# Scaled attention output in a second buffer, and the first two row blocks of the pooling difference split into a place of their own

## What is computed

```python
h = rms_norm(x, norm_mix)
q, k, v, u, ga, gp = jnp.split(h @ w_in, SPLITS, axis=-1)
o = attention_fn(q, k, v, lam)                                # (b, t, 8 heads, 128)
o = (rms_norm(o, head_norm) * (1.0 - lam_init)).reshape(b, t, ATTN_WIDTH)
pool_o, pool_state = pool_mixer(u, pool_prefix, p0, w_pool, pool_scale)
merged = jax.nn.sigmoid(ga) * (o @ w_attn_branch) + jax.nn.sigmoid(gp) * (pool_o @ w_pool_branch)
x1 = x + merged @ w_out

def pool_mixer(...):            # for each of 4 groups of 256 channels, window w = 2, 4, 8, 16
    d = ((hi - lo) / cnt - ext[...]).astype(u.dtype)          # mean of the window minus the token
    outs.append(jnp.einsum('btc,cd->btd', d, w_pool[g]) * pool_scale[g])
```

## Time and profile before

| | us |
|---|---|
| median of 3 runs | 2158.81 (2157.7 to 2162.5) |
| the profiled execution, its own time | 2162.38 |
| its span, first to last instruction | 2160.6 |
| TensorE busy | 2096.9 (97%) |
| mean granted TensorE clock | 0.994 |

### The profile page before, as it was taken

The page is one execution under the profiler, slowest core; times in us unless marked ns, Lnnn a source line. Parts: engine busy times, 40 slices in busy tenths (PEclk is TensorE's granted clock), DMA queues, the critical chain, the costliest instruction groups (busy, mean ns, idle before and its releaser), DMA issues.

```text
span 2160.6 us, 34490 instructions
## 1 busy us (share of the span) xinstructions
PE 2096.9 (97%) x13501; PEld 1907.2 (88%) x13501; DVE 1067.6 (49%) x1389; ACT 671.2 (31%) x1322; POOL 503.2 (23%) x382
## 2 busy tenths in 40 slices
PE   6999999999999999999999999999999999999998
PEld 6788888888888887899999887999999899999996
DVE  5566667666310101266773433555555555555555
ACT  4344454444443333224112311311221122122120
POOL 5423333332010101332331100311221221122120
PEclk9999999999999999999999999999999999999999
DMA  5222111222367886211124420201110111111112
GB/s 154 58 56 58 40 55 34 56 60 75 126 225 269 285 279 221 84 50 55 59 78 130 123 88 1 70 20 60 50 40 30 54 55 41 31 49 60 31 39 94
DMA packets 174539, 186.00 MB, mean 86 GB/s; under 512 B 8239, under 2 KB 147259, under 8 KB 174402
## 3 DMA queue, kind: packets, MB, share of 16 engines
q1 hardware_dynamic: 163786, 175.21, 26.0%
q10 hardware_dynamic: 10624, 8.92, 1.2%
HBM read 161.09 MB, written 23.24 MB: 85 GB/s over the span
## 4 chain that ended last, share of the span: by engine, by line
PE 85%; issue 6%; DVE 3%; POOL 2%; DMA 1%; ACT 1%; SPq 0%; ACTq 0%; POOLq 0%; DVEq 0%
PE PS L1362 33%; PE PS L2017 12%; PE PS L913 8%; PE PS L279 4%; PE PS L281 4%; PE PS L280 4%; PE PS L1839 4%; PE PS L313 3%; PE PS L337 3%; PE PS L968 3%; PE PS L326 2%; PE PS L983 2%; PE PS L1022 1%; POOL fw_lo L1349 1%; PE PS L292 1%
## 5 line engine op out<-in xcount | busy, mean ns | idle before, releaser
L1349 POOL TENSOR_TENSOR fw_lo<-fw_raw,fw_hi 128x1024 fp32r<-128x1024 f32 x86 | 215.7, 2508 | 883.0 <-ACT fw_hi L1345 838.4
L1362 PE MATMUL PS<-m_hi,fw_hi 128*128 128x384 f32 (+1 forms) x1032 | 228.4, 329 | 3.1 <-issue 1.8
L1362 PE MATMUL PS<-m_lo,fw_hi 128*128 128x384 f32 (+1 forms) x1032 | 227.4, 328 | 0.0
L1362 PE MATMUL PS<-m_hi,fw_lo 128*128 128x384 f32 (+1 forms) x1032 | 227.4, 328 | 0.0
L2144 DVE TENSOR_TENSOR x<-x,PS 128x512 f32<-128x512 f32 x198 | 135.9, 688 | 141.0 <-PE PS L2017 140.9
L279 PE MATMUL PS<-w_hi,act_hi 128*128 128x384 f32 (+1 forms) x520 | 188.2, 362 | 0.0
L1362 PEld LDWEIGHTS PS<-m_hi,fw_hi 128*128 128x128 f32 x1032 | 175.8, 188 | 4.1 <-issue 2.4
L281 PE MATMUL PS<-w_hi,act_lo 128*128 128x384 f32 (+1 forms) x520 | 176.7, 340 | 0.0
L1362 PEld LDWEIGHTS PS<-m_hi,fw_lo 128*128 128x128 f32 x1032 | 176.3, 188 | 0.0
L1362 PEld LDWEIGHTS PS<-m_lo,fw_hi 128*128 128x128 f32 x1032 | 176.2, 188 | 0.0
L280 PE MATMUL PS<-w_lo,act_hi 128*128 128x384 f32 (+1 forms) x520 | 176.1, 339 | 0.0
(11 more groups left out here) (261 smaller groups left out, 4288.5 us busy)
## 6 DMA issues: line engine op xcount, KB each, us to landing
k_pg<-in_cache_k_dram SPq DMA_DIRECT2D x64, 512.0 KB, 4.8
v_pg<-in_cache_v_dram SPq DMA_DIRECT2D x64, 512.0 KB, 5.2
fw_raw<-in_w_up_dram SPq DMA_DIRECT2D x44, 512.0 KB, 4.1
fw_raw<-in_w_in_dram SPq DMA_DIRECT2D x24, 512.0 KB, 4.8
wd_raw<-in_w_down_dram SPq DMA_DIRECT2D x22, 512.0 KB, 4.1
w_raw<-in_w_in_dram SPq DMA_DIRECT2D x21, 512.0 KB, 5.3
out_dram<-raw SPq DMA_DIRECT2D x16, 512.0 KB, 3.7
ga_scratch<-ga_ring ACTq DMA_DIRECT2D x8, 544.0 KB, 7.1
```

The source lines that it names most:

```text
L1349: e.tensor_tensor(fw_lo[slot][:, 0:kts, :], fw_raw[:, 0:kts, :], fw_hi[slot][:, 0:kts, :].bitcast(F32), ALU.subtract).then_inc(fw_tail, 1)
L1362: ins = e.matmul(PS[:, 3 * slot + c, 0:cw], w[slot][:, kt, :], x[:, kt, c0:c0 + cw], start=first and kt == 0, stop=last and kt == KT - 1)
```

## The change

Three things are done.

1. `d_first`, a pair of buffers (hi and lo) of two row blocks each, is placed in the region of the u buffers. Row blocks 0 and 1 of dT are split into it and not over `act_hi` / `act_lo`; TensorE's pool map reads them there.
2. ACT's copies of these two blocks are put ahead of the last gate (they stay behind `fm_head(N_PL)`), and DVE's subtractions of them are put ahead of `dve_normalize_o(0)`. The wait on the stores of the pooling state (`ur_st`) moves ahead of the first write to `po_lo`.
3. The scaled attention output goes to `o_sq`; the transposes read `o_sq`, and SP waits for `scaled_o` in place of `o_tr` before it loads the next block.

```diff
+        D_FIRST = 2
+        d_first = [at(f"d_first{i}", [P, D_FIRST, TOK], F32R, R2U + fit(TOK) + i * fit(D_FIRST, TOK)) for i in range(2)]
...
+        def d_parts_of(kt):
+
+            return d_first if kt < D_FIRST else (act_hi, act_lo)
...
                 e.wait_ge(d_tail, kt + 1)
-                for w, x, first, last in ((w_h, act_hi, True, False), (w_h, act_lo, False, False), (w_l, act_hi, False, True)):
+                d_hi, d_lo = d_parts_of(kt)
+                for w, x, first, last in ((w_h, d_hi, True, False), (w_h, d_lo, False, False), (w_l, d_hi, False, True)):
...
-                    ins = e.transpose(PS[:, 6 + half, j * P:j * P + n_rows], o_tile[0:n_rows, h * P:(h + 1) * P],
+                    ins = e.transpose(PS[:, 6 + half, j * P:j * P + n_rows], o_sq[0:n_rows, h * P:(h + 1) * P],
...
-            gate(N_GP + 1, KT - 1, 1)
-            e.wait_ge(d_done, KT)
...
-                    e.activation(act_hi[:, kt, :], dT[:, kt, :], ACT.Copy).then_inc(d_head, 1)
-
-            d_parts(range(5))
+                    e.activation(d_parts_of(kt)[0][:, kt, :], dT[:, kt, :], ACT.Copy).then_inc(d_head, 1)
+
+            e.wait_ge(d_done, KT)
+            d_parts(range(D_FIRST))
+            gate(N_GP + 1, KT - 1, 1)
+            d_parts(range(D_FIRST, 5))
...
-            v = o.rearrange("p (h d) -> p h d", h=NH)
-            e.tensor_tensor(v, v, rst[0:n_rows, 0, 0:NH].unsqueeze(2).to_broadcast([n_rows, NH, VD]), ALU.mult).then_inc(scaled_o, 1)
+            v, scaled = [x[0:n_rows, :].rearrange("p (h d) -> p h d", h=NH) for x in (o_tile, o_sq)]
+            e.tensor_tensor(scaled, v, rst[0:n_rows, 0, 0:NH].unsqueeze(2).to_broadcast([n_rows, NH, VD]), ALU.mult).then_inc(scaled_o, 1)
...
                 dve_pool_tile(e, step, m)
+            for kt in range(D_FIRST):
+                dve_d_tail(e, kt)
             dve_normalize_o(e, step, 0, NSAMP)
+            for kt in range(D_FIRST, 5):
+                dve_d_tail(e, kt)
             e.wait_ge(ur_st, UR_STORES * 16)
-            for kt in range(5):
-                dve_d_tail(e, kt)
...
             with e.Fori(0, KT - 1) as i:
-                e.wait_ge(o_tr, i * 2 + 2)
+                e.wait_ge(scaled_o, i + 1)
                 e.dma_start(o_tile[:, :], o_dram[bass.ds(i * P, P), :]).then_inc(o_ld, 16)
...
-            e.wait_ge(o_tr, 2 * TT - 2)
+            e.wait_ge(scaled_o, TT - 1)
             e.dma_start(o_tile[:, :], o_dram[SEQ - P:SEQ, :]).then_inc(o_ld, 16)
```

More of the change, by code:

```diff
@@ L1679, in dve_d_tail @@
             e.wait_ge(d_head, kt + 1)
-            e.tensor_tensor(act_lo[:, kt, :], dT[:, kt, :], act_hi[:, kt, :].bitcast(F32),
+            d_hi, d_lo = d_parts_of(kt)
+            e.tensor_tensor(d_lo[:, kt, :], dT[:, kt, :], d_hi[:, kt, :].bitcast(F32),
                             ALU.subtract).then_inc(d_tail, 1)
```

## The result

| | before | after |
|---|---|---|
| median, 11 runs each | 2160.81 us (2156.85 to 2166.34) | 2166.81 us (2164.77 to 2170.43) |
| span of the profiled execution | 2160.6 | 2165.1 |
| mean granted clock | 0.994 | 0.993 |

The changed kernel takes 1.0025 times as long (95% interval 1.0014 to 1.0035), 5.4 us more by that ratio; the two medians lie 6.0 us apart. The forecast was 2165.7 and +6.9. All ratios are of fast executions; one of the twelve of e4_copies_first, 2933.7 us long at a mean granted clock of 0.655, is slow and left out.

A forecast was written before the change was run, and what follows sets the result against it. TensorE, busy for 97% of the span, was taken as the bound. Pool map +6.0, clock +0.9 and early load 0 gave +6.9 us, added to the 2158.8 median: 2165.7 us, range 2161.0 to 2168.6.

The forecast's parts named there:

- The chain on DVE: Sample block: two subtractions follow ACT's copies and end at 997.8; normalization starts then, 14.0 us later, its scaling at 1002.6.
- The meeting with POOL: Sample block's scaling on DVE runs into POOL's fw_lo and takes 3.41 us in place of 1.22.
- Start of the transposes: Sample block's transposes on TensorE start at 1006.05 in place of 996.84; the pool map at 1006.65, +6.0 us.
- The clock: Half clock behind TensorE's gap loses 2.4 us, against 1.5 behind the present gap: +0.9, bounds 0 and +3.3.
- The early load: Prompt-block loop: SP issues the o_tile load 1.3 us sooner, but nobody waits for it: 0 us.
- The sum: Whole kernel: +6.0 for the pool map, +0.9 for the clock, 0 for the load: +6.9 us, 2165.7 us.
- the loop is not bound by the load: Denies the rival that the load bound the prompt-block loop and TensorE's 3.5 us of waits could go: 2162.2, 7%.
- POOL and DVE do meet: Denies the rival that they don't meet at the sample block's scaling as in the loop: 2164.0 to 2165.2 us, 12%.
- The one in which the change does what it is shaped for: Rival: subtractions and normalization done by 996.8, pool map at 997.5, no half clock: 2154.2 us, chance 4%.
- its condition: For that rival, ACT's w_pool hi part must begin at 987.0 for an equally early pool map; rows show 993.09.

The follow-up runs named there:

- e4_copies_first: Changed kernel with the sample block's normalization ahead of dT's subtractions on DVE, and ACT's two d_first copies ahead of w_pool's hi part; ratio to before 0.9975.
- e7: Kernel before with one wait added: in the prompt-block loop POOL begins each fw_lo only when DVE has scaled the block; ratio to before 0.9989.
- e10: Kernel before with POOL's fw_lo put ahead of the root in the loop over prompt blocks; ratio to before 0.9999.
- e3_norm_first: Changed kernel with the sample block's normalization put ahead of the subtractions of dT on DVE again; ratio to before 0.9980.

## Why the prediction was right

Step by step, counted from ACT's hi part of w_pool:

- *The chain on DVE.* The copies, the subtractions and the normalization follow as forecast: the square starts after 4.50 us (4.7 forecast), the scaling 4.77 us later, as in the earlier trace rows.
- *The meeting with POOL.* 3.35 us, 3.41 forecast; POOL came first by 0.07 us again, and the run with fw_lo ahead of the root shows that the meeting is its cause. All nine scalings of the kernel after are between 3.35 and 3.42 us.
- *Start of the transposes.* After 12.72 us, 12.96 forecast; the pool map after 13.73, 13.56 forecast, since the transposes themselves ran at half clock and took 1.0 and not 0.6 us.
- *The clock.* 2.6 us in this execution, 2.4 forecast. The 2.4 came from the kernel's start, another place, and that it fits is in part luck. What I subtracted for the kernel before, 1.5, was 1.6 in its profile (47.28 against 45.70 in the run with the output kept beside), but this is not a fixed price. In that run the gap in front of the pool map was 3.07 us too and no half clock came behind it:

```profile
1000.66 0.73 PE L1378 MATMUL PS<-act_hi,fw_hi 128*128 128x384 f32 x3 [3.07 <-DVE act_lo L1680]
...
1001.72 0.66 PE L1378 MATMUL PS<-act_hi,fw_lo 128*128 128x384 f32 x3
1002.22 0.66 PE L1378 MATMUL PS<-act_hi,fw_hi 128*128 128x384 f32 x3
```

  In the profile of before the same matmuls are 0.9 us apart, and so they are in the two other runs that keep this gap, e7 and e10 (their first block comes at 45.8 all the same, since the wait ahead of its transposes is gone). The price behind the long gap varies as well: 54.16 and 53.25 us to the first block in two executions with the same order. In both the clock was down for some 10 us, but it fell 4.5 us ahead of the transposes in the first and 6.5 in the second, so that 5.7 and 3.7 us of work met half clock. So the term was right for the two profiled executions that it compares; over the profiles at hand it is 0 or about 1.5 before and 1.6 to 2.6 after, and what decides within that is not shown.
- *The early load.* 0 forecast and 0 measured. One reading on the way was wrong: that ACT needs the weights load behind `o_tile` only 5 us later. ACT stands idle for it in the kernel before,

```profile
1047.05 1.06 ACT L1345 ACTIVATE fw_hi<-fw_raw 128x1024 fp32r<-128x1024 f32 x1 [3.06 <-DMA fw_raw<-in_w_pool_branch_dram]
```

  and it costs nothing there only because POOL makes the root ahead of fw_lo. With the other order on POOL this load is what decides.
- *The sum.* 6.9 us at the first block, as forecast; 4.5 in the two spans, with 1.5 us gained ahead of the change's place and 0.9 behind it, in stretches with the same work. The ratio's interval is 3.0 to 7.6 us. That the forecast time, 2165.7, is only 1.1 us from the median of 2166.81 is luck in part: it was added to the median of three runs, 2158.81, which is 2.0 us below that of the eleven, and the forecast difference is 0.9 us above that of the medians.

The rivals that were tested fell: the loop is not bound by the load, POOL and DVE do meet. The one in which the change does what it is shaped for was priced about right: the run with the copies first gains 5.4 us, and the 4.6 forecast for that case is within its interval. But its condition was too narrow. It named only the moment at which ACT begins with w_pool's hi part, and e3_norm_first gains 4.3 us with that moment unchanged, by the order on DVE alone. No run has an earlier hi part with DVE's order as changed.

## What to carry to other kernels

A step that is put ahead of another on an in-order engine brings its own wait with it: before splitting a wait off, look at what releases the moved instruction (here ACT behind a weight load), and at how much slack the instructions behind it had (here 7 us, all of it used). A loop that waits for one engine can be held up by a second one whose instructions exclude the first one's, and which of the two orders is better depends on when the data for them is loaded. An edit that is worth nothing alone can be what another one needs.

## What the runs showed of the hardware

- A POOL subtraction of two SBUF inputs and a DVE instruction of two SBUF inputs did not run at once in any of the rows read here: DVE took 3.35 to 3.42 us in place of 1.22 where POOL's 2.40 us began first, and POOL took 3.29 in place of 2.40 where DVE's square began first. DVE's reduction (one input) ran beside it at its usual 1.22 us.
- The same gap of 3.07 us on TensorE was followed by half clock in three profiles and by none in one; it cost about 1.5 us or nothing.
- A product of 128 by 128 by 128 in full fp32 took 0.22 to 0.23 us (18.0 for 80, 9.5 for 42), and they kept the clock up over the gap; eight transposes of the same size take 1.09 with the last one's way through the array.
